# Output projections and down-projections finished tile by tile, with the norms of finished tiles in half rows between products of later tiles

## Chip, cores and metric

One core of one Trainium2 chip. The metric is the device time in microseconds of one execution, as the median of several runs of the same program; lower is better.

## What is computed

A decoder trunk of two layers over 512 tokens of width 1024, float32. Every sub-layer is `x + post_norm(f(pre_norm(x)))` with RMS norms over the 1024 columns; f is a mixer (recurrent heads in layer 0, sparse attention in layer 1) or a squared-ReLU MLP of width 4096. Cut to what matters here:

```python
def rmsnorm(x, w):
    return x * lax.rsqrt(jnp.mean(x * x, axis=-1, keepdims=True) + 1e-6) * w
x = x + rmsnorm(mixer(rmsnorm(x, pre_mix)) @ w_out, post_mix)       # w_out 1024 x 1024
u = rmsnorm(x, pre_ffn)
x = x + rmsnorm(jnp.square(relu(u @ w_up)) @ w_down, post_ffn)      # 1024 x 4096, 4096 x 1024
```

## The kernel before

Tokens stand in four tiles of 128 partitions (i = 0 to 3, NT); the residual is `xres`. Every large product is made of three float32r products (`mm3`, L307 to L311): each operand is split into a high part (ACT copies it, rounding) and a low part (DVE subtracts the high part). SyncE streams 200 weight chunks of 128 x 1024 (512 KB) into a ring of four slots; a slot is loaded again when its chunk's low part has been made (`w_lo`, `stream`). `split_hi` (ACT, L294) and `split_lo` (DVE, L302) make `wh` and `wl`, also four slots each; they wait until PE has used the chunk four places earlier (`w_used`).

The program is a row of stages, each written for every engine separately and in fixed order; `meet` is a barrier of PE, ACT, DVE and POOL between them. Inside a stage each engine runs its own list in order and waits on semaphores. `Chain.link` and `Chain.sig` also make an engine wait for its own last result.

- `oproj_pe` (L1376): for every one of eight chunks k, all four tiles and both halves of 512 columns, so 24 products a chunk into eight PSUM banks (bank 2i + h for tile i, half h). All tiles end in the last chunk.
- `post_act`, `post_dve` (L376, L385): the post-norm of a tile, whole rows: ACT squares and sums `ffo[i]` and takes the root; DVE takes the reciprocal, scales by it and the row `rowbuf` (L393) and adds to `xres` (L395).
- `norm_act`, `norm_dve`, `norm_pe` (L337, L355, L318): the pre-norm: ACT squares `xres[i]` and takes the root, DVE writes `utok` (L365, two buffers), PE turns it by eight 128 x 128 transposes (L328), ACT and DVE write high and low parts `uh`, `ul` (L342, L360).
- `first_hi`, `first_lo`: the next stage's first two chunks are split behind that.
- `mlp_pe`, `mlp_act`, `mlp_dve` (L1441 to L1524): two passes (`it`) over half of the 4096 hidden columns each. Each pass has 16 chunks of up-projection (24 products each), then eight chunks of down-projection for the left 512 output columns in banks 4 to 7 and eight for the right ones in banks 0 to 3, every chunk for all four tiles; DVE adds the banks into `ffo`, which POOL cleared before (L2064, L2075). Only inside the last chunk do the tiles end one after another.

The four places that the prediction speaks of are: output projection of layer 0 to its MLP; end of that MLP to the input projection of layer 1 (`proj1`, operands `uh`, `ul`, `wh`, `wl` of its own, `D1`, of which the input part lies over buffers that the MLP uses); output projection of layer 1 to its MLP; end of that MLP to the output. `DM` names the MLP's and output projection's four operand buffers.

Of the kernel before, what the change touches and what calls it, by code (L numbers as in the profile page):

```python
# [29 lines left out]
P = 128  # L30
# [115 lines left out]
def program(nc, wstream, x, pos, params, consts, rows, out):  # L146
    with ExitStack() as ctx:
# [22 lines left out]
        st = sb("st", [P, 32])  # L170
# [76 lines left out]
        utok = sb("utok", [P, 2, D], c=ml)  # L247
        sb("rest", [P, 2 * HF * T - 2 * D], c=ml)
# [4 lines left out]
        DM = [uh_m, ul_m, wh_m, wl_m]  # L253
        hraw = sb("hraw", [P, 2, T], c=ml)
# [36 lines left out]
        def split_hi(a, dn, c, it=0, per=0):  # L291
            a.e.wait_ge(slot_sems[c % RING], it * (16 * per // RING) + 16 * (c // RING + 1))
            a.e.wait_ge(sem("w_used"), it * per + c + 1)
            a.sig(a.e.activation(dn[2][:, c % RING, :], slot(c), ACT.Copy), sem("w_hi"), it * per + c + 1)  # L294
# [20 lines left out]
        NORM_TURN = (0, 2, 3, 5)  # L315


        def norm_pe(pe, c, ut):  # L318
            if c == 2:
                pe.wait_ge(sem("right_out"), 12)  # L320
            elif c % 2:

                pe.wait_ge(sem("ffo_left"), 4 * (c // 2) + 4)
                pe.wait_ge(sem("ffo_right"), 4 * (c // 2) + 4)
            for i in range(NT):
                pe.wait_ge(sem("norm_u"), 4 * c + i + 1)
# [10 lines left out]
        def norm_act(a, c, dn, ut):  # L337
            def high(i):
                a.e.wait_ge(sem("turned"), 4 * NORM_TURN[c] + i + 1)
                for h in range(2):  # L340
                    hi, _, src = turned(dn, i, h)
                    a.sig(a.e.activation(hi, src, ACT.Copy), sem("high_done"), 8 * NORM_TURN[c] + 2 * i + h + 1)  # L342
            for i in range(NT):
                if c > 0:
                    a.e.wait_ge(sem("x_updated"), 4 * (c - 1) + i + 1)
                if i >= 2:
                    a.e.wait_ge(sem("turned"), 4 * NORM_TURN[c] + i - 1)
                a.link(a.e.activation(ut[:, i % 2, :], xres[:, i, :], ACT.Square, accum_out=st[:, i:i + 1]))
                a.sig(a.e.activation(st[:, 4 + i:5 + i], st[:, i:i + 1], ACT.Sqrt, bias=eps, scale=1.0 / D),
                      sem("norm_root"), 4 * c + i + 1)  # L350
# [4 lines left out]
        def norm_dve(v, c, dn, ut, row):  # L355
            def low(i):
                for h in range(2):
                    hi, lo, src = turned(dn, i, h)
                    v.e.wait_ge(sem("high_done"), 8 * NORM_TURN[c] + 2 * i + h + 1)
                    v.link(v.e.tensor_tensor(lo, src, hi.bitcast(F32), ALU.subtract))  # L360
            v.e.wait_ge(sem("pre_loaded"), 16 * (c + 1))
            for i in range(NT):
                v.e.wait_ge(sem("norm_root"), 4 * c + i + 1)
                v.link(v.e.reciprocal(st[:, 8 + i:9 + i], st[:, 4 + i:5 + i]))
                v.sig(v.e.scalar_tensor_tensor(ut[:, i % 2, :], xres[:, i, :], st[:, 8 + i:9 + i], row[:, :], ALU.mult, ALU.mult),  # L365
                      sem("norm_u"), 4 * c + i + 1)
# [6 lines left out]

        def post_act(a, c, ready, scratch):  # L376
            for i in range(NT):
                ready(i)
                if i >= 2:
                    a.e.wait_ge(sem("post_root"), 4 * c + i - 1)  # L380
                a.link(a.e.activation(scratch(i), ffo[:, i, :], ACT.Square, accum_out=st[:, 16 + i:17 + i]))
                a.sig(a.e.activation(st[:, 20 + i:21 + i], st[:, 16 + i:17 + i], ACT.Sqrt, bias=eps, scale=1.0 / D),
                      sem("post_root"), 4 * c + i + 1)

        def post_dve(v, c, ready):  # L385
            v.e.wait_ge(sem("row_loaded"), 16 * (c + 1))
            ready(0)
            for i in range(NT):
                if i + 1 < NT:
                    ready(i + 1)  # L390
                v.e.wait_ge(sem("post_root"), 4 * c + i + 1)
                v.link(v.e.reciprocal(st[:, 24 + i:25 + i], st[:, 20 + i:21 + i]))
                v.link(v.e.scalar_tensor_tensor(ffo[:, i, :], ffo[:, i, :], st[:, 24 + i:25 + i], rowbuf[:, :],  # L393
                                                ALU.mult, ALU.mult))
                v.sig(v.e.tensor_tensor(xres[:, i, :], xres[:, i, :], ffo[:, i, :], ALU.add),  # L395
                      sem("x_updated"), 4 * c + i + 1)

# [975 lines left out]
        def oproj_pe(pe, first):  # L1376
            mh, ml_, wh, wl = DM
            for k in range(KD):
                c = first + k
                weights(pe, c)  # L1380
                for i in range(NT):
                    if k == KD - 1 and i > 0:
                        ins.then_inc(sem("tile_done"), 1)
                    t = slice(i * P, (i + 1) * P)
                    for h in range(2):
                        w = slice(h * 512, (h + 1) * 512)
                        ins = mm3(pe, bank[2 * i + h][:, :], mh[:, k, t], ml_[:, k, t], wh[:, c % RING, w], wl[:, c % RING, w], k == 0, k == KD - 1)
                ins.then_inc(sem("w_used"), 1)

        def row_in(act, r):  # L1390
            act.dma_start(rowbuf[:, :], rows[r:r + 1, :].to_broadcast([P, D])).then_inc(sem("row_loaded"), 16)

        def oproj_act(a, c, first):
            if c == 0:

                a.e.dma_start(xres[:, :, :], x_d).then_inc(sem("aux_loaded"), 16)
            row_in(a.e, 2 * c)
            pre_in(a.e, 2 * c + 1, prerow)
            for k in range(KD):
                split_hi(a, DM, first + k)  # L1400

            def ready(i):
                if i < NT - 1:
# [869 lines left out]
```

## Time and profile before

| | |
|---|---|
| median of 3 runs | 1752.99 us (1751.8 to 1754.39) |
| the profiled execution | 1752.1 us, of which 1750.3 us span |
| mean granted TensorE clock | 0.931 of full speed |
| PE, DVE, ACT, POOL busy | 87%, 49%, 38%, 6% of the span |
| DMA | 119.42 MB, mean 68 GB/s |

Busy time is a share over the whole program. The timeline lists instructions in order of start with their length; what stands in brackets is how long the engine had been idle before and which instruction on which engine released it. Products overlap: each is recorded with 0.39 us, and the distance of two starts is what one costs. PEclk is the granted TensorE clock, 1.0 being the upper level (2.4 GHz) and 0.5 the lower (1.2 GHz).

### The profile page before, as it was taken

How to read it: one execution, taken by the hardware profiler on the slowest of the kernel's cores; microseconds unless marked ns; L12 is line 12 of the kernel's file. 1: busy time of each engine (PE TensorE's matmuls, PEld its weight loads, DVE VectorE, ACT ScalarE, POOL GpSimd, SP SyncE). 2: the span in 40 equal slices, each digit the busy share in tenths (PEclk: the TensorE clock that was granted, in tenths of full speed). 3: DMA queues.
4: the chain of work that ended last, by engine and by line, in shares of the span. 5: the costliest groups of instructions: out<-in, count | busy, mean ns of one | idle time of the engine just before them, and what ended most of it. 6: DMA issues, size and time to landing. Idle time of an engine off the chain costs nothing.

```text
span 1750.3 us, 22860 instructions
## 1 busy us (share of the span) xinstructions
PE 1528.7 (87%) x8817; PEld 1269.1 (73%) x8817; DVE 864.4 (49%) x1356; ACT 663.4 (38%) x1116; POOL 99.1 (6%) x133
## 2 busy tenths in 40 slices
PE   3999988998929499999997796779979599999996
PEld 2776766887828388888885685669977488888885
DVE  3366636656481644224424425577761644224423
ACT  3544413444441444114412324347762444124411
POOL 0100012212150000000000000000000000000000
PEclk8999988999959699999999797789989699999998
DMA  5222200000023223222321231200011123322321
GB/s 193 73 79 78 73 0 1 1 1 1 8 106 116 72 95 110 97 83 94 113 97 37 72 97 47 73 1 2 2 57 65 60 97 109 96 85 96 109 84 48
DMA packets 32260, 119.42 MB, mean 68 GB/s; under 512 B 3616, under 2 KB 3616, under 8 KB 32032
## 3 DMA queue, kind: packets, MB, share of 16 engines
q1 hardware_dynamic: 29616, 109.10, 18.9%
q10 hardware_dynamic: 2544, 8.92, 1.4%
q8 instruction: 71, 1.16, 0.3%
q14 instruction: 29, 0.24, 0.0%
HBM read 115.91 MB, written 2.10 MB: 67 GB/s over the span
## 4 chain that ended last, share of the span: by engine, by line
PE 57%; DVE 6%; ACT 2%; issue 1%; ACTq 0%; DVEq 0%
PE bank L309 16%; PE bank L310 16%; PE bank L311 16%; PE bank L1928 2%; PE bank L1941 2%; PE bank L1918 1%; PE bank L1917 1%; PE bank L1777 1%; DVE ffo L393 1%; DVE xres L395 1%; PE bank L1807 1%; PE bank L1919 1%; PE bank L328 0%; PE bank L1823 0%; DVE utok L365 0%
## 5 line engine op out<-in xcount | busy, mean ns | idle before, releaser
L302 DVE TENSOR_TENSOR wl_m<-ring,wh_m 128x1024 fp32r<-128x1024 f32 x144 | 176.5, 1226 | 226.5 <-ACT wh_m L294 225.2
L294 ACT ACTIVATE wh_m<-ring 128x1024 fp32r<-128x1024 f32 x144 | 152.8, 1061 | 278.2 <-PE bank L311 264.4
L309 PE MATMUL bank<-uh_m,wh_m 128*128 128x512 f32 x512 | 201.3, 393 | 12.5 <-DVEq L1496 10.6
L310 PE MATMUL bank<-ul_m,wh_m 128*128 128x512 f32 x512 | 200.7, 392 | 0.0
L311 PE MATMUL bank<-uh_m,wl_m 128*128 128x512 f32 x512 | 200.4, 391 | 0.0
L309 PE MATMUL bank<-wh_m,hh 128*128 128x512 f32 x512 | 199.2, 389 | 0.0
L310 PE MATMUL bank<-wl_m,hh 128*128 128x512 f32 x512 | 199.2, 389 | 0.0
L311 PE MATMUL bank<-wh_m,hl 128*128 128x512 f32 x512 | 199.2, 389 | 0.0
L1505 DVE TENSOR_TENSOR hraw<-hraw 128x512 f32<-128x512 f32 x64 | 44.3, 693 | 171.0 <-ACT hraw L1483 171.0
L1483 ACT ACTIVATE hraw<-bank 128x512 f32<-128x512 f32 x64 | 38.3, 598 | 221.9 <-PE bank L311 221.9
L309 PEld LDWEIGHTS bank<-uh_m,wh_m 128*128 128x128 f32 x512 | 97.0, 189 | 34.1 <-POOLq L259 5.7
L311 PEld LDWEIGHTS bank<-uh_m,wl_m 128*128 128x128 f32 x512 | 97.1, 190 | 20.4
L310 PEld LDWEIGHTS bank<-ul_m,wh_m 128*128 128x128 f32 x512 | 97.1, 190 | 20.2
L311 PEld LDWEIGHTS bank<-wh_m,hl 128*128 128x128 f32 x512 | 96.1, 188 | 20.0
L309 PEld LDWEIGHTS bank<-wh_m,hh 128*128 128x128 f32 x512 | 96.1, 188 | 19.9
L310 PEld LDWEIGHTS bank<-wl_m,hh 128*128 128x128 f32 x512 | 96.1, 188 | 19.9
L302 DVE TENSOR_TENSOR wl<-ring,wh 128x1024 fp32r<-128x1024 f32 x47 | 58.1, 1236 | 105.7 <-ACT wh L294 105.5
L309 PE MATMUL bank<-uh,wh 128*128 128x512 f32 x216 | 87.9, 407 | 5.1 <-DVEq L259 5.1
L310 PE MATMUL bank<-ul,wh 128*128 128x512 f32 x216 | 85.4, 395 | 0.0
L311 PE MATMUL bank<-uh,wl 128*128 128x512 f32 x216 | 85.4, 395 | 0.0
L1975 ACT ACTIVATE pb<-bank,nmax 128x128 f32<-128x128 f32 (+3 forms) x128 | 64.3, 530 | 27.9 <-DVE nmax L1991 27.4
L328 PE MATMUL bank<-con,utok 128*128 128x128 f32 x96 | 21.6, 409 | 52.8 <-DVE utok L365 52.8
(380 smaller groups left out, 2799.0 us busy)
## 6 DMA issues: line engine op xcount, KB each, us to landing
ring<-in_wstream_dram SPq DMA_DIRECT2D x200, 512.0 KB, 3.4
rowbuf<-in_rows_dram ACTq DMA_DIRECT2D x6, 512.0 KB, 6.9
xres<-in_x_dram SPq DMA_DIRECT2D x1, 2048.0 KB, 12.0
xres<-in_x_dram ACTq DMA_DIRECT2D x1, 2048.0 KB, 7.4
out_dram<-xres ACTq DMA_DIRECT2D x4, 512.0 KB, 3.2
prerow<-in_rows_dram ACTq DMA_DIRECT2D x3, 512.0 KB, 8.4
con<-in_consts_dram SPq DMA_DIRECT2D x1, 1127.5 KB, 7.4
par<-in_params_dram SPq DMA_DIRECT2D x1, 955.5 KB, 13.9
```

The costliest lines, as they stand in the source:

```text
L294: a.sig(a.e.activation(dn[2][:, c % RING, :], slot(c), ACT.Copy), sem("w_hi"), it * per + c + 1)
L302: v.sig(v.e.tensor_tensor(dn[3][:, c % RING, :], slot(c), dn[2][:, c % RING, :].bitcast(F32), ALU.subtract), sem("w_lo"), it * per + c + 1)
L309: pe.matmul(out, lh, rh, start=start, stop=False)
L310: pe.matmul(out, lh, rl, start=False, stop=False)
L311: return pe.matmul(out, ll, rh, start=False, stop=stop)
L328: ins = pe.transpose(bank[2 * i + k // 4][:, (k % 4) * P:(k % 4 + 1) * P], ut[:, i % 2, k * P:(k + 1) * P], ident)
L393: v.link(v.e.scalar_tensor_tensor(ffo[:, i, :], ffo[:, i, :], st[:, 24 + i:25 + i], rowbuf[:, :], ALU.mult, ALU.mult))
L1483: a.sig(e.activation(hraw[:, s % 2, :], bank[s % 4][:, :], ACT.Relu), sem("relu_done"), it * HF + (hb + s + 1))
L1505: v.sig(e.tensor_tensor(h, h, h, ALU.mult), sem("h_sq"), it * HF + (hb + s + 1))
L1928: ins = pe.transpose(bank[4 + i % 2][:, k * P:(k + 1) * P], pb[:, i, k * P:(k + 1) * P], ident)
L1941: ins = pe.matmul(bank[6 + b][r:r + 64, i * (HD + 1):(i + 1) * (HD + 1)], pT[:, g % 2, c:c + 64], vx[:, k, b, h % KG, :], start=(k == 0), ...
L1975: e.activation(pb[:, i, 0:w], bank[i][:, 0:w], ACT.Exp, bias=nmax[:, g % 2, i:i + 1]).then_inc(sem("p_sb"), 1)
```

## The change

1. Output projection: all eight chunks stay split in memory (`o_weights`: four in `DM`, four in new buffers `wh_o`, `wl_o` over the hidden activations' place). PE makes tiles 0 and 1 over all chunks, then tile 2, then the left half of tile 3, then transposes tiles 0 and 1, then the right half of tile 3, then transposes tiles 2 and 3.
2. The last half of each down-projection (right columns, second pass) likewise: the last four of eight chunks are split into `DD`, the memory of `uh_m` and `ul_m`. Tiles 0 and 1, tile 2, (first MLP: transposes of 0 and 1), tile 3, (transposes of 2 and 3).
3. Norms in half rows: ACT squares 512 columns at a time, for an output projection straight out of PSUM; an Identity step turns the first half's sum into the bias of the root over the second half's. DVE multiplies by `rowbuf` without waiting for the root, and one scalar_tensor_tensor per half scales by 1/root and adds to `xres`. The copy of the output projection into `ffo` goes. `ffo` takes the place of `utok`.
4. Both next chunks' splits stand inside the last tile's norm. POOL's clearings of `ffo` go; the first pass copies the banks instead of adding them.

The core of it:

```diff
+        def turn_tile(pe, n, i):
+            for h in range(2):
+                pe.wait_ge(sem("u_new"), 8 * n + 2 * i + h + 1)
+                for q in range(4):
+                    ins = pe.transpose(bank[TURN_BANK[n][i] + h][:, q * P:(q + 1) * P], ffo[:, i, (4 * h + q) * P:(4 * h + q + 1) * P], ident)
+                ins.then_inc(sem("n_turned"), 1)
+
+        def post_half(a, i, h, src, event, value):
+
+            a.sig(a.e.activation(hraw[:, h, :], src, ACT.Square, accum_out=ST(4 + h, i)), sem(event), value)
+            if h == 0:
+                a.link(a.e.activation(ST(6, i), ST(4, i), ACT.Identity, bias=eps, scale=1.0 / D))
...
+        def x_out(v, n, i, scaled):
+            v.e.wait_ge(sem("post_root"), 4 * n + i + 1)
+            v.link(v.e.reciprocal(ST(8, i), ST(7, i)))
+            for h in range(2):
+                x = xres[:, i, half(h)]
+                v.sig(v.e.scalar_tensor_tensor(x, scaled(i, h), ST(8, i), x, ALU.mult, ALU.add), sem("x_new"), 8 * n + 2 * i + h + 1)
...
             for k in range(KD):
-                c = first + k
-                weights(pe, c)
-                for i in range(NT):
-                    if k == KD - 1 and i > 0:
+                weights(pe, first + k)
+                for i in range(2):
+                    for h in range(2):
+                        ins = product(i, h, k)
+                    if k == KD - 1:
                         ins.then_inc(sem("tile_done"), 1)
...
+            for h in range(2):
+                for k in range(KD):
+                    ins = product(2, h, k)
+            ins.then_inc(sem("tile_done"), 1)
             for k in range(KD):
+                ins = product(3, 0, k)
+            ins.then_inc(sem("tile_done"), 1)
+            turn_tile(pe, n, 0)
+            turn_tile(pe, n, 1)
             for k in range(KD):
+                product(3, 1, k).then_inc(sem("w_used"), 1)
+            turn_tile(pe, n, 2)
+            turn_tile(pe, n, 3)
...
+            post(0)
+            post(1)
+            pre_root(a, n, 0)
+            pre_root(a, n, 1)
+            post(2)
+            pre_root(a, n, 2)
+            high_out(a, DM, n, 0)
+            high_out(a, DM, n, 1)
+            post(3)
+            for c in range(2):
+                split_hi(a, DM, first + KD + c)
+            pre_root(a, n, 3)
+            high_out(a, DM, n, 2)
+            high_out(a, DM, n, 3)
...
+            for f in range(HF):
+                ins = down(2, f, 2, first + HF + J + f // 2, d_weights(f // 2))
+            ins.then_inc(sem("tile_done"), 1)
+            if c == 0:
+                turn_tile(pe, 1, 0)
+                turn_tile(pe, 1, 1)
+            for f in range(HF):
+                ins = down(3, f, 3, first + HF + J + f // 2, d_weights(f // 2))
+                if f % 2:
+                    ins.then_inc(sem("w_used"), 1)
...
+            post(3)
+            if c == 0:
+                used(e, first + 2 * MB - 1)
+                high_out(a, D1, n, 0)
+                high_out(a, D1, n, 1)
+                pre_root(a, n, 3)
+                for k in range(2):
+                    split_hi(a, D1, C_IN1 + k)
+                high_out(a, D1, n, 2)
+                high_out(a, D1, n, 3)
...
+            def scale(i):
+                r = ffo[:, i, half(1)]
+                d_ready(e, first, c, i)
+                v.sig(e.tensor_tensor(r, bank[i][:, :], r, ALU.add), sem("right_sum"), 4 * c + i + 1)
+                v.link(e.tensor_tensor(scaled(i, 1), r, rowbuf[:, half(1)], ALU.mult))
...
-            pool.wait_ge(sem("x_updated"), 4)
-            g.link(pool.memset(ffo[:, :, :], 0.0))
```

PE at the first output projection's end, before: the last products (`uh_m` is here the mixer's output), all transposes, the first products of the MLP.

```order
L309 MATMUL bank<-wh_m,uh_m 128x512
L310 MATMUL bank<-wl_m,uh_m 128x512
L311 MATMUL bank<-wh_m,ul_m 128x512
L328 MATMUL bank<-con,utok 128x128 x32
L309 MATMUL bank<-uh_m,wh_m 128x512
L310 MATMUL bank<-ul_m,wh_m 128x512
L311 MATMUL bank<-uh_m,wl_m 128x512
```

The same stage on PE after the change, the transposes of tiles 0 and 1 with their neighbours:

```order
L313 MATMUL bank<-wl_o,uh_m 128x512
L314 MATMUL bank<-wh_o,ul_m 128x512
L386 MATMUL bank<-con,ffo 128x128 x16
L312 MATMUL bank<-wh_m,uh_m 128x512
L313 MATMUL bank<-wl_m,uh_m 128x512
L314 MATMUL bank<-wh_m,ul_m 128x512
```

And the transposes of tiles 2 and 3, between the last product and the MLP's first:

```order
L313 MATMUL bank<-wl_o,uh_m 128x512
L314 MATMUL bank<-wh_o,ul_m 128x512
L386 MATMUL bank<-con,ffo 128x128 x16
L312 MATMUL bank<-uh_m,wh_m 128x512
L313 MATMUL bank<-ul_m,wh_m 128x512
```

Sixteen of the 32 transposes have moved in front of the last 24 products; sixteen stay behind them.

DVE there, before, from the last tile's post-norm (L392 to L395) through the pre-norms (L365), the low parts (L360) and the splits (L302):

```order
L392 RECIPROCAL st<-st 128x1
L393 SCALAR_TENSOR_TENSOR ffo<-ffo,st,rowbuf 128x1024
L395 TENSOR_TENSOR xres<-xres,ffo 128x1024
L364 RECIPROCAL st<-st 128x1
L365 SCALAR_TENSOR_TENSOR utok<-xres,st,prerow 128x1024
L364 RECIPROCAL st<-st 128x1
L365 SCALAR_TENSOR_TENSOR utok<-xres,st,prerow 128x1024
L360 TENSOR_TENSOR ul_m<-bank,uh_m 128x4x128 x2
L364 RECIPROCAL st<-st 128x1
L365 SCALAR_TENSOR_TENSOR utok<-xres,st,prerow 128x1024
L360 TENSOR_TENSOR ul_m<-bank,uh_m 128x4x128 x2
L364 RECIPROCAL st<-st 128x1
```

After the change, from the last pre-norm step of tile 2 (L425) to the end of the stage:

```order
L425 SCALAR_TENSOR_TENSOR ffo<-xres,st,prerow 128x512 x2
L432 TENSOR_TENSOR ul_m<-bank,uh_m 128x4x128 x4
L1492 TENSOR_TENSOR ffo<-bank,rowbuf 128x512 x2
L305 TENSOR_TENSOR wl_m<-ring,wh_m 128x1024
L416 RECIPROCAL st<-st 128x1
L419 SCALAR_TENSOR_TENSOR xres<-ffo,st,xres 128x512 x2
L305 TENSOR_TENSOR wl_m<-ring,wh_m 128x1024
L423 RECIPROCAL st<-st 128x1
L425 SCALAR_TENSOR_TENSOR ffo<-xres,st,prerow 128x512 x2
L432 TENSOR_TENSOR ul_m<-bank,uh_m 128x4x128 x4
```

The post-norms and pre-norms of three tiles and the low parts of two stand ahead of the last tile's scaling (L1492); behind it are the last tile's x (L419) and u (L425), both weight splits, and four low parts (L432).

DVE at the first MLP's end, after the change (L1670 adds the right half, L1671 multiplies it by the row into PSUM):

```order
L1670 TENSOR_TENSOR ffo<-bank,ffo 128x512
L1671 TENSOR_TENSOR bank<-ffo,rowbuf 128x512
L416 RECIPROCAL st<-st 128x1
L419 SCALAR_TENSOR_TENSOR xres<-ffo,st,xres 128x512
L419 SCALAR_TENSOR_TENSOR xres<-bank,st,xres 128x512
L432 TENSOR_TENSOR ul<-bank,uh 128x4x128 x4
L423 RECIPROCAL st<-st 128x1
L425 SCALAR_TENSOR_TENSOR ffo<-xres,st,prerow 128x512 x2
L305 TENSOR_TENSOR wl<-ring,wh 128x1024 x2
L432 TENSOR_TENSOR ul<-bank,uh 128x4x128 x4
```

Here all eight low parts (L432) stand behind the last tile's sum, where the order before is that of the output projection's end, with the buffers of `D1`.

## Rows read from the trace of the kernel before

**Rows 1.** Page, parts 1 (busy us, share, instructions) and 4 (chain by engine)

```profile
PE 1528.7 (87%) x8817; PEld 1269.1 (73%) x8817; DVE 864.4 (49%) x1356; ACT 663.4 (38%) x1116; POOL 99.1 (6%) x133
...
PE 57%; DVE 6%; ACT 2%; issue 1%; ACTq 0%; DVEq 0%
```

**Rows 2.** Waits of PE: engine line waited for: us in total, times, longest us

```profile
PE bank L328 <- DVE utok L365: 52.8, 9, 14.5
...
PE bank L309 <- DVEq L1496: 10.6, 2, 5.3
```

**Rows 3.** Timeline of PE, first output projection to MLP: start, length, operation

```profile
568.05 0.39 PE L310 MATMUL bank<-wl_m,uh_m 128*128 128x512 f32 x1
568.28 0.39 PE L311 MATMUL bank<-wh_m,ul_m 128*128 128x512 f32 x1
...
581.89 3.65 PE L328 MATMUL bank<-con,utok 128*128 128x128 f32 x16 [13.22 <-DVE utok L365]
...
588.30 1.10 PE L328 MATMUL bank<-con,utok 128*128 128x128 f32 x8 [2.77 <-DVE utok L365]
...
591.27 1.97 PE L328 MATMUL bank<-con,utok 128*128 128x128 f32 x8 [1.87 <-DVE utok L365]
...
598.54 0.76 PE L309 MATMUL bank<-uh_m,wh_m 128*128 128x512 f32 x1 [5.30 <-DVEq L1496]
...
603.33 0.40 PE L311 MATMUL bank<-uh_m,wl_m 128*128 128x512 f32 x1
```

**Rows 4.** Timeline of PE, around first MLP's end and second output projection's end

```profile
949.99 0.39 PE L311 MATMUL bank<-wh_m,hl 128*128 128x512 f32 x1
...
979.44 0.79 PE L309 MATMUL bank<-wh,uh 128*128 128x512 f32 x1 [5.10 <-DVEq L259]
...
1353.37 0.39 PE L311 MATMUL bank<-wh_m,ul_m 128*128 128x512 f32 x1
...
1384.92 0.76 PE L309 MATMUL bank<-uh_m,wh_m 128*128 128x512 f32 x1 [5.30 <-DVEq L1496]
```

**Rows 5.** Timelines of PE and DVE, the end of the program

```profile
1735.80 0.39 PE L311 MATMUL bank<-wh_m,hl 128*128 128x512 f32 x1
...
1745.91 1.23 DVE L395 TENSOR_TENSOR xres<-xres,ffo 128x1024 f32<-128x1024 f32 x1
```

**Rows 6.** Windows of the first gap: us, then busy us by engine, PEclk, DMA

```profile
568.70:582.00 13.30, 0.11 (x1) 0.14 (x2) 12.75 (x17) 7.36 (x17) 1.66 (x1) 0.64 0.00 0
582.00:594.00 12.00, 6.61 (x32) 5.57 (x32) 8.31 (x11) 7.11 (x14) 1.86 (x1) 0.64 0.01 2
```

**Rows 7.** Timeline of ACT, first output projection's norms and splits

```profile
565.51 1.06 ACT L381 ACTIVATE utok<-ffo 128x1024 f32<-128x1024 f32 x1 [0.23 <-DVE ffo L1422]
...
566.69 0.29 ACT L382 ACTIVATE st<-st,con 128x1 f32<-128x1 f32 x1
...
583.93 1.23 ACT L342 ACTIVATE uh_m<-bank 128x512 fp32r<-128x512 f32 x2 [4.68 <-PE bank L328]
...
594.59 2.14 ACT L294 ACTIVATE wh_m<-ring 128x1024 fp32r<-128x1024 f32 x2
```

**Rows 8.** Timeline of DVE, same place and the half rows just before

```profile
511.85 0.75 DVE L1359 SCALAR_TENSOR_TENSOR ul_m<-bank,par,uh_m 128x512 fp32r<-128x512 f32 x1
...
567.70 0.17 DVE L392 RECIPROCAL st<-st 128x1 f32<-128x1 f32 x1 [0.93 <-ACT ffo L1407]
...
584.63 1.42 DVE L360 TENSOR_TENSOR ul_m<-bank,uh_m 128x512 fp32r<-128x512 f32 x2 [1.36 <-ACT uh_m L342]
...
595.75 2.48 DVE L302 TENSOR_TENSOR wl_m<-ring,wh_m 128x1024 fp32r<-128x1024 f32 x2 [0.30 <-ACT wh_m L294]
```

**Rows 9.** Weight ring from 521 to 540 us: issue to landing

```profile
DMA to landing us min/median/max: 3.3/7.6/7.6
```

**Rows 10.** Timeline of DVE, last MLP, behind the left half's products

```profile
1692.77 2.87 DVE L1516 TENSOR_TENSOR ffo<-bank,ffo 128x512 f32<-128x512 f32 x4 [8.48 <-PE bank L311]
1695.67 2.48 DVE L302 TENSOR_TENSOR wl_m<-ring,wh_m 128x1024 fp32r<-128x1024 f32 x2
```

More of the change, by code:

```diff
@@ L353, in norm_act, with norm_dve @@
             high(NT - 1)
[L355 removed]
+        def norm_dve(v, dn, ut, row):
             def low(i):
@@ L385, in post_dve, with row_in @@
[L385 to L396, printed above, removed]
+        def row_in(act, r):
+            act.dma_start(rowbuf[:, :], rows[r:r + 1, :].to_broadcast([P, D])).then_inc(sem("row_loaded"), 16)
@@ new lines, in u_out, with low_out @@
+        def u_out(v, n, i):
+            v.e.wait_ge(sem("pre_root"), 4 * n + i + 1)
+            v.link(v.e.reciprocal(ST(13, i), ST(12, i)))
+            for h in range(2):
+                v.sig(v.e.scalar_tensor_tensor(ffo[:, i, half(h)], xres[:, i, half(h)], ST(13, i), prerow[:, half(h)], ALU.mult, ALU.mult),
+                      sem("u_new"), 8 * n + 2 * i + h + 1)
+        def low_out(v, dn, n, i):
+            for h in range(2):
+                hi, lo, src = renorm_out(dn, n, i, h)
+                v.e.wait_ge(sem("n_high"), 8 * n + 2 * i + h + 1)
+                v.link(v.e.tensor_tensor(lo, src, hi.bitcast(F32), ALU.subtract))
@@ new lines, in mlp_pe @@
+                for j in range(J):
+                    ch = first + HF + j
+                    weights(pe, ch, it, MB)
+                    pe.wait_ge(sem("h_lo"), it * HF + (2 * HF * c + 2 * j + 2))
+                    for f in (2 * j, 2 * j + 1):
+                        for i in range(NT):
+                            ins = down(i, f, 4 + i, ch)
+                    ins.then_inc(sem("w_used"), 1)
+                for j in range(J):
+                    ch = first + HF + J + j
+                    weights(pe, ch, it, MB)
+                    for f in (2 * j, 2 * j + 1):
+                        for i in range(NT if it == 0 else 2):
+                            ins = down(i, f, i, ch, d_weights(j) if it else None)
+                            if it == 1 and f == HF - 1:
@@ L1509, in mlp_dve @@
                         e.sem_inc(sem("hraw_free"), 1)
[L1510 to L1511 removed]
+                    for right, end in ((0, HF + J - 1), (1, MB - 1)):
+                        if s == end:
                             used(e, first + s, it, MB)
                             for i in range(NT):
[L1514 to L1516 removed]
@@ new lines, in mlp_dve @@
+                                if right:
+                                    v.sig(ins, sem("right_out"), 8 * c + 4 + i + 1)
+                                else:
+                                    v.sig(ins, sem("left_out"), it * 4 + (12 * c + 4 + i + 1))
+            for j in range(2, J):
+                split_lo(v, [None, None] + list(d_weights(j)), first + HF + J + j, 1, MB)
+            e.wait_ge(sem("row_loaded"), 16 * (n + 1))
+            for i in range(NT):
+                e.wait_ge(sem("left_sq"), 4 * c + i + 1)
+                v.link(e.tensor_tensor(ffo[:, i, half(0)], ffo[:, i, half(0)], rowbuf[:, half(0)], ALU.mult))
```

318 lines of the change are left out of this document (182 added, 136 removed).

## The prediction

> **What bounds the kernel now.** I read the page first. TensorE (PE) is busy for 1528.7 of 1750.3 us and the chain that ended last is 57% PE, nearly all of it in the three-product helper [rows 1]: in the large products nothing but PE sets the time. Then the list of PE's waits. Its longest total, 52.8 us in 9 waits, is for the token rows that VectorE (DVE) writes in the pre-norm, and 10.6 us more is for the stage barrier that follows [rows 2]. The timeline shows where that lies. At the end of the first output projection the last product starts at 568.28 and the first product of the MLP at 598.54, 30.26 us later; between them PE does 32 transposes and otherwise waits [rows 3]. The same gap is 979.44 - 949.99 = 29.45 us after the first MLP and 1384.92 - 1353.37 = 31.55 us after the second output projection [rows 4]. After the last MLP there is no product left: 1750.3 - 1735.80 = 14.5 us from the last product's start to the end of the span [rows 5]. Together 105.8 us, in which DVE works almost without a break (12.75 of 13.30 us in the first part of the first gap [rows 6]). So the four junctions are bound by DVE and ScalarE (ACT), and products are bound by PE: the change can only win by putting junction work beside products.
>
> **The prices.** Two products in succession start 0.227 us apart at full clock (568.05, 568.28) [rows 3]. ACT: a square of a whole row with its sum 1.18 (565.51 to 566.69, when the root starts), the root 0.29, so 0.33 with the handover [rows 7]; two half rows out of PSUM 1.23, so 0.63 each, and two weight splits 2.14, so 1.08 each with the handover. DVE: a reciprocal 0.17; two half-row subtractions 1.42, so 0.73 each; a half-row scalar_tensor_tensor 0.75, so 0.78; two weight splits 2.48, so 1.24 each [rows 8]. A square of a half row is not in the trace: it lies between 0.62 (a half-row copy) and 1.18 (the whole row with its sum), and I take 0.78: the whole-row square alone (1.06) is as long as a whole-row split (1.07), so half a row should be near the half-row copy, and the sum comes on top. DVE writing its product into PSUM (the right half of the down-projection) isn't there either: the nearest row is the half-row subtraction that reads PSUM, 0.73; I take that, and twice that as the upper bound; nothing there excludes a little less.
>
> **Inside the products: what is added to PE.** Sixteen of the 32 transposes of each of the three junctions now stand between products. Eight took 1.10 us at full clock and 1.97 at half [rows 3]; after products the clock is full, so 16 cost 2.2 us (upper bound 4.0). The product count is unchanged, only the order. Three junctions: 6.6 us added.
>
> Do tiles 0 and 1 reach these transposes in time? In the output projection DVE has four scalings (2.9), and per tile two passes of reciprocal and two half rows (2 x 2 x 1.76 = 7.0), plus about 1.2 of waiting for ACT: 11.1 us after tile 1's last product, while PE has 48 + 24 products, 16.3 us, in front of the transposes. In the down-projection it is 9.9 us against 48 products, 10.9 us. No stall, though the second margin is thin.
>
> Do the weights come in time? A chunk now lasts 12 products, 2.7 us, in the passes over tiles 0 and 1, where it lasted 24 (5.4). Splits take 1.24 a chunk on DVE. In the worst window a refill landed 7.6 us after its issue [rows 9]; with four slots that is (7.6 + 1.1 + 1.2) / 4 = 2.5 us a chunk. In the down-projection DVE first adds four left halves, then splits the third chunk: 2.9 + 1.3 = 4.2 us after the left products ended (1692.77 to 1696.9 in this trace [rows 10]), needed at 5.4. So nothing is added. The two clearings of ffo on POOL go; they lay beside the junctions. The first accumulation becomes a copy at the same length. ACT's extra work (small Identity steps, two per tile at 0.33) falls mostly beside products. Each costs nothing while PE is in products.
>
> **The junctions after the change**, from the last product's start (its result is usable about 0.5 us later).
>
> Output projection (twice). ACT's last square 0.8 to 1.3, root to 1.7, first split to 2.7. DVE's second split half waits for that and ends at 4.0; then reciprocal and x in two halves to 5.8. The second weight split keeps DVE until 7.05; beside it ACT squares both halves of x and takes the root, to 7.0. Reciprocal and two half rows: 8.8. PE transposes the first half from about 8.1, both by 10.3, at half clock. ACT's high part of the second half to 11.0, DVE's low part to about 12.1, barrier and first product 0.3: **12.4 us**. Gain: 30.26 - 12.4 - 2.2 = 15.7 in the first, 31.55 - 12.4 - 2.2 = 16.95 in the second (there a table load also leaves the exposed part).
>
> First MLP. The buffer for the next layer's input overlaps the weights in use, so the high and low parts of tiles 0 to 2 may only start after the last product, and DVE is the bound: sum and scaling 1.45, wait for the root 0.5, reciprocal and x 1.76, low parts of tiles 0 and 1 2.9, reciprocal and u 1.76, two splits 2.5, low parts of tiles 2 and 3 2.9: 13.8, with the start and barrier **14.6 us**. Gain 29.45 - 14.6 - 2.2 = 12.65.
>
> End of the program. Sum 0.73, square 0.78 (beside the scaling), root 0.33, reciprocal 0.2, two half rows 1.56, handovers: 4.2 us from the last product's start, then the output transfer as now, from 1747.14 to 1750.3, 3.2 [rows 5]: **7.4 us**, gain 7.1.
>
> Sum: 15.7 + 16.95 + 12.65 + 7.1 = 52.4 us. The profiled execution took 1752.1, which gives 1699.7; the median is 0.9 higher, 1752.99, which gives **1700.6 us**.
>
> The clock at the restarts I leave as it is. After the gap the products start at half clock: 11 intervals took 4.79 us (598.54 to 603.33) where full clock needs 2.5 [rows 3], 2.3 us lost per junction. The first such start came after 5.30 us without work on PE; the new gaps still hold some 6 us of it, and about 2 more before the first product.
>
> **A rule against the change.** In the stretch from 582 to 594 us PE did only transposes, and the granted clock averaged 0.64 there; eight of them ran at 1.10 us after 16 others [rows 3, 6]. So in this trace the clock rose on transposes alone. The Trainium skill (TensorE: Matmul & The Clock Gate, Part 4: PE-mode transpose) says the opposite, that transpose-mode work doesn't count as PE being busy and the full clock doesn't engage. By the rule the transposes between products would work like idle time; by the row they don't.
>
> **Rivals.**
> 1. The 16 transposes among products drop the clock and the products behind them restart at half: three times 2.3 = 6.9 us lost, 1707.5. For: PE goes from dense products to short operations, and what one such interruption does to the clock the trace doesn't show. Against: the clock rose on transposes, and in the 13.3 us after the last product, with nothing on PE, it still averaged 0.64 [rows 6], so it did not fall at once. This is what the skill's rule above would bring. Chance 0.08.
> 2. The shorter gaps keep the clock up to the next products: 6.9 us won, 1693.7. For: transposes right behind the last product, and a gap of 12 where it was 30. Against: 6 us of silence in its middle, where 5.30 us were followed by a start at half clock. 0.08.
> 3. The pieces don't fit beside the products as walked: the half-row chain is slower (squares at 1.18, four per tile, handovers), PE stands at the in-line transposes of the MLP, and the tails grow. With 0.5 us more on each of some five path squares or writes per junction, and 1 to 2 us of standing in the first MLP, 10 us less is won: 1710.6. It would also be what one sees if the norm work didn't overlap as the change says. 0.10.
> 4. Slower than before: the weights become the bound. Four passes take 8 chunks each at half the old time per chunk. It decides from 52.4 / 32 = 1.64 us of lateness per chunk, 4.3 us in place of 2.7, a refill round of 17 us over the four slots; at 19 us (4.75 a chunk, 2.05 late) it costs 66 us: 1766. For: 3.1 MB of x and rows load during the first of these passes. Against: 7.6 us was the slowest landing even then, and half of the chunks are loaded before the pass begins. 0.02.
>
> **Numbers.** The forecast as walked has 0.72. Its unknown costs: up to 0.7 us for writing PSUM at two ends, 0.4 more for some three exposed squares at each of four junctions (4.8), 1.8 for each set of in-line transposes (5.4): upper end 1700.6 + 1.4 + 4.8 + 5.4 = 1712; with not all at once, and the rivals 1 and 3, I close at 1711. The lower end takes in rival 2, 1693.7, so 1694. A measurement of this kernel can tell about 0.2% (3.5 us) from no change; all cases but the last and a piece of it lie far below: faster 0.97, same 0.01, slower 0.02.
>
> **What would show it.** Right: PE's gaps between the last product and the next stage near 12.4, 14.6 and 12.4 us and 7.4 at the end; two groups of 16 transposes at each junction, the first within products and about 2.2 us long; no PE wait for split weights inside the two-tile passes; DVE in the first MLP's gap without a break. Wrong: products at 0.427 us pitch behind the in-line transposes (rival 1), full clock from the first product of a stage (2), a wait of PE for ffo ahead of the in-line transposes or gaps over 15 us (3), waits for the split weights (4). If the gaps agree and the time doesn't, the order of products has a price that I set at nothing.

## The result and the profile after

| | before | after |
|---|---|---|
| median | 1753.03 us (4 runs) | 1701.57 us (4 runs, 1701.43 to 1702.56) |
| ratio, 95% interval | | 0.9707 [0.9691, 0.9724] |
| span of the profiled execution | 1750.3 us | 1699.7 us |
| mean granted clock | 0.931 | 0.948 |

The forecast was 1700.6 us, with a range from 1694 to 1711. Busy times and the last chain by engine, from the page (answers to [rows 1]; the chain shown is the one from the last instruction back and here reaches less far):

```profile
PE 1522.0 (90%) x8817; PEld 1263.8 (74%) x8817; DVE 868.5 (51%) x1392; ACT 674.4 (40%) x1192; POOL 91.6 (5%) x131
...
PE 23%; DVE 1%; ACT 0%; issue 0%; ACTq 0%; DVEq 0%
```

PE is busy for 6.7 us less in a span that is 50.6 us shorter. Its waits for the token rows and for the stage barrier (answers to [rows 2]; engine, line, waited for: us in total, times, longest):

```profile
PE bank L386 <- DVE ffo L425: 20.8, 3, 7.0
...
PE bank L312 <- DVEq L1634: 3.9, 2, 2.0
```

52.8 us in nine waits have become 20.8 in three, and 10.6 at the barrier 3.9. Timeline of PE around the first output projection's end (answers to [rows 3]):

```profile
565.49 0.40 PE L314 MATMUL bank<-wh_o,ul_m 128*128 128x512 f32 x1
565.72 1.91 PE L386 MATMUL bank<-con,ffo 128*128 128x128 f32 x16
567.38 0.48 PE L312 MATMUL bank<-wh_m,uh_m 128*128 128x512 f32 x1
567.70 0.39 PE L313 MATMUL bank<-wl_m,uh_m 128*128 128x512 f32 x1
...
572.73 0.39 PE L314 MATMUL bank<-wh_o,ul_m 128*128 128x512 f32 x1
572.96 1.04 PE L386 MATMUL bank<-con,ffo 128*128 128x128 f32 x8
580.96 1.97 PE L386 MATMUL bank<-con,ffo 128*128 128x128 f32 x8 [6.97 <-DVE ffo L425]
584.90 0.77 PE L312 MATMUL bank<-uh_m,wh_m 128*128 128x512 f32 x1 [1.97 <-DVEq L1634]
...
588.38 0.40 PE L314 MATMUL bank<-uh_m,wl_m 128*128 128x512 f32 x1
```

Sixteen transposes stand among the products and move the next product from 565.72 to 567.38, by 1.66 us. The products behind them are at full clock at once. From the last product's start (572.73) to the MLP's first (584.90) it is 12.17 us, where it was 30.26. The start is at half clock again: eight intervals until 588.38 took 3.48 us.

PE at the first MLP's end and at the second output projection's end (answers to [rows 4]):

```profile
937.53 0.39 PE L314 MATMUL bank<-uh_m,hl 128*128 128x512 f32 x1
...
951.91 0.79 PE L312 MATMUL bank<-wh,uh 128*128 128x512 f32 x1 [4.29 <-DVEq L261]
...
1327.49 0.39 PE L314 MATMUL bank<-wh_o,ul_m 128*128 128x512 f32 x1
...
1339.66 0.76 PE L312 MATMUL bank<-uh_m,wh_m 128*128 128x512 f32 x1 [1.97 <-DVEq L1634]
```

951.91 - 937.53 = 14.38 us (29.45 before) and 1339.66 - 1327.49 = 12.17 us (31.55). The window from the last product to the last tile's first transposes in the first gap (us, then busy us of PE, PEld, DVE, ACT, POOL, PEclk, DMA share; answers to [rows 6]):

```profile
573.00:581.00 8.00, 1.03 (x10) 0.80 (x8) 5.78 (x9) 6.21 (x13) 0.00 (x0) 0.82 0.21 71
```

DVE is busy for 5.78 of 8.00 us and ACT for 6.21, where DVE had 12.75 of 13.30 and ACT 7.36: what is left is one tile's chain to and fro between them.

ACT in the pass over tiles 0 and 1 (the fifth chunk's split) and at the last half row of tile 3 (answers to [rows 7]):

```profile
532.18 1.06 ACT L297 ACTIVATE wh_o<-ring 128x1024 fp32r<-128x1024 f32 x1 [5.29 <-DMA ring<-in_wstream_dram]
...
573.22 0.60 ACT L391 ACTIVATE hraw<-bank 128x512 f32<-128x512 f32 x1 [3.27 <-PE bank L314]
...
573.94 0.29 ACT L396 ACTIVATE st<-st 128x1 f32<-128x1 f32 x1
```

The fifth chunk's split came when its transfer landed, 532.18, and PE first used that chunk at 538.51: the weights were in time. A half-row square took 0.60, and the root started 0.72 after it. DVE from the last half row on (answers to [rows 8]):

```profile
574.00 0.69 DVE L1492 TENSOR_TENSOR ffo<-bank,rowbuf 128x512 f32<-128x512 f32 x1 [2.26 <-ACT hraw L391]
575.42 1.23 DVE L305 TENSOR_TENSOR wl_m<-ring,wh_m 128x1024 fp32r<-128x1024 f32 x1 [0.72 <-ACT wh_m L297]
576.68 0.16 DVE L416 RECIPROCAL st<-st 128x1 f32<-128x1 f32 x1
576.88 1.54 DVE L419 SCALAR_TENSOR_TENSOR xres<-ffo,st,xres 128x512 f32<-128x512 f32 x2
578.45 1.22 DVE L305 TENSOR_TENSOR wl_m<-ring,wh_m 128x1024 fp32r<-128x1024 f32 x1
```

Between the scaling (574.00) and the reciprocal (576.68) stands a weight split that waits for ACT's half of it. The end of the program (answers to [rows 5]):

```profile
1690.31 0.39 PE L314 MATMUL bank<-uh_m,hl 128*128 128x512 f32 x1
...
1691.53 0.70 DVE L1671 TENSOR_TENSOR bank<-ffo,rowbuf 128x512 f32<-128x512 f32 x1
...
1693.73 0.75 DVE L419 SCALAR_TENSOR_TENSOR xres<-bank,st,xres 128x512 f32<-128x512 f32 x1
...
1692.67 2.91 ACTq L2311 DMA_DIRECT2D out_dram<-xres  x4
```

The last product starts at 1690.31, the span ends at 1699.7: 9.39 us, not 7.4. DVE is done at 1694.48 and has kept to the forecast (4.17 us after the last product's start, forecast 4.2). But ScalarE issued all four output transfers between 1692.67 and 1695.6: they stand in its list behind the last root. Before, they stood behind the last root too:

```profile
1743.17 4.34 ACTq L2158 DMA_DIRECT2D out_dram<-xres  x4
```

From the first issue to the end of the span it was 7.1 us then (1743.17 to 1750.3), and it is 7.0 us now.

### The profile page after: what moved, and what is told of

It reads as the page before. It is cut to its first block and busy times, and to the rows that moved or that the text cites. A ratio compares the mean times of both kernels' runs of the same rounds, so it can differ in the third digit from the quotient of the medians.

```text
span 1699.7 us, 22980 instructions
## 1 busy us (share of the span) xinstructions
PE 1522.0 (90%) x8817; PEld 1263.8 (74%) x8817; DVE 868.5 (51%) x1392; ACT 674.4 (40%) x1192; POOL 91.6 (5%) x131
## 5 line engine op out<-in xcount | busy, mean ns | idle before, releaser
L305 DVE TENSOR_TENSOR wl_m<-ring,wh_m 128x1024 fp32r<-128x1024 f32 x128 | 156.9, 1226 | 161.5 <-ACT wh_m L297 160.3
L297 ACT ACTIVATE wh_m<-ring 128x1024 fp32r<-128x1024 f32 x128 | 135.8, 1061 | 202.0 <-PE bank L314 189.3
L312 PE MATMUL bank<-wh_m,hh 128*128 128x512 f32 x448 | 174.4, 389 | 0.0
L314 PE MATMUL bank<-wh_m,hl 128*128 128x512 f32 x448 | 174.3, 389 | 0.0
L313 PE MATMUL bank<-wl_m,hh 128*128 128x512 f32 x448 | 174.3, 389 | 0.0
L314 PEld LDWEIGHTS bank<-wh_m,hl 128*128 128x128 f32 x448 | 84.1, 188 | 17.6
L313 PEld LDWEIGHTS bank<-wl_m,hh 128*128 128x128 f32 x448 | 84.1, 188 | 17.4
L312 PEld LDWEIGHTS bank<-wh_m,hh 128*128 128x128 f32 x448 | 84.1, 188 | 17.4
L312 PE MATMUL bank<-wh,uh 128*128 128x512 f32 (+1 forms) x160 | 62.0, 387 | 4.3 <-DVEq L261 4.3
```

The lines of the kernel that those rows point to most:

```text
L305: v.sig(v.e.tensor_tensor(dn[3][:, c % RING, :], slot(c), dn[2][:, c % RING, :].bitcast(F32), ALU.subtract), sem("w_lo"), it * per + c + 1)
L312: pe.matmul(out, lh, rh, start=start, stop=False)
L313: pe.matmul(out, lh, rl, start=False, stop=False)
L314: return pe.matmul(out, ll, rh, start=False, stop=stop)
```

## The experiments

Gaps below are from the start of a stage's last product to the start of the next stage's first. All times compare with the kernel before, run on the same chip beside it.

**1. Tiles together again in the output projections.**

```diff
             for k in range(KD):
                 weights(pe, first + k)
-                for i in range(2):
+                for i in range(NT):
                     for h in range(2):
                         ins = product(i, h, k)
...
+                ins.then_inc(sem("w_used"), 1)
+            for i in range(NT):
+                turn_tile(pe, n, i)
```

> Output projections only: PE goes back to all four tiles chunk by chunk, transposes all behind the last product; the half-row norms and the MLP stay as changed. Theory (the gain is work moved beside products, half rows by themselves win little): the gap from the last product's start to the MLP's first rises from 12.2 to about 29 us at both places, minus 1.7 us for the transposes that leave the products: +15.3 us each, near 1732 us. Rival (the gain is that half-row norms have a shorter chain, whatever the order of products): the gap stays under 20 us, +3 to +12 us in all, 1705 to 1714.

Measured 1732.44 us, ratio 0.9877 [0.9862, 0.9892]. PE:

```profile
570.91 0.39 PE L314 MATMUL bank<-wh_o,ul_m 128*128 128x512 f32 x1
576.53 3.87 PE L386 MATMUL bank<-con,ffo 128*128 128x128 f32 x16 [5.23 <-DVE ffo L425]
584.91 1.97 PE L386 MATMUL bank<-con,ffo 128*128 128x128 f32 x8 [4.52 <-DVE ffo L425]
595.57 1.97 PE L386 MATMUL bank<-con,ffo 128*128 128x128 f32 x8 [8.69 <-DVE ffo L425]
599.51 0.76 PE L312 MATMUL bank<-uh_m,wh_m 128*128 128x512 f32 x1 [1.97 <-DVEq L1624]
```

The gap is 599.51 - 570.91 = 28.60 us; at the second place it is 1370.85 - 1340.96 = 29.89. So half rows as such, with the new order inside ACT's and DVE's lists, take 1.66 us off either gap (30.26, 31.55; the second is 1.29 longer in both kernels, where a table load of ScalarE, 1.28 us, stands just ahead of it). The rest of the gain there comes from the order of products, by which the norms of three tiles run beside products. The rival falls. The same was not tried at the first MLP's end: how much of its 15.07 us is half rows and how much is order is not shown.

**2. Outputs issued by SyncE.**

```diff
             stream(sp)
+            for i in range(NT):
+                sp.wait_ge(sem("x_new"), 24 + 2 * i + 2)
+                sp.dma_start(out_d[:, i, :], xres[:, i, :]).then_inc(sem("x_moved"), 16)
...
-            for i in range(NT):
-                act.wait_ge(sem("x_new"), 24 + 2 * i + 2)
-                act.dma_start(out_d[:, i, :], xres[:, i, :]).then_inc(sem("x_moved"), 16)
```

> The four output transfers are issued by SyncE, each as soon as its tile of x is ready, in place of by ScalarE behind its last root. Theory (the tail of 9.4 us, 2.0 over what was forecast, is the 2 MB that all start moving only at 1692.7): the tail falls to about 7.2 us, time 1699.5. Rival (the tail is the fixed cost of the last transfer and its wait): tail stays at 9.4, 1701.6.

Measured 1699.47 us, 0.9695 [0.9681, 0.9708]. PE's last product, and the four issues (1672.30 is the first, the second number the stretch to the end of the last):

```profile
1689.56 0.39 PE L314 MATMUL bank<-uh_m,hl 128*128 128x512 f32 x1
...
1672.30 21.79 SPq L2218 DMA_DIRECT2D out_dram<-xres  x4
```

The span ends at 1696.9, 7.34 us after the last product's start. A transfer lands 2.7 us after its issue at the median, where it was 4.0 with all four at once. That accounts for the 2.05 us by which the tail was too long: it was bound by 2.1 MB, which in the changed kernel moved at 401 to 418 GB/s from 1694 to 1698, so in some 5 us, and could not start before ScalarE came to them. The gap shows this, not the median: the unaltered kernel did not run beside this one, and the runs scatter from 1697.26 to 1700.95 us.

**3. The MLP's in-line transposes behind the last product.**

```diff
             ins.then_inc(sem("tile_done"), 1)
-            if c == 0:
-                turn_tile(pe, 1, 0)
-                turn_tile(pe, 1, 1)
             for f in range(HF):
...
             if c == 0:
-                turn_tile(pe, 1, 2)
-                turn_tile(pe, 1, 3)
+                for i in range(NT):
+                    turn_tile(pe, 1, i)
```

> First MLP only: the 16 transposes of tiles 0 and 1 stand behind the last product instead of before tile 3. Theory (behind it DVE is the bound and PE waits about 7 us, so they are free there, and cost 1.7 us among the products): gap from last product to next stage unchanged at 14.4, time 1699.9. Rival (the high parts start later and everything shifts): gap longer by 1.7 or more, 1701.6 or above.

Measured 1700.34 us (five runs, 1696.16 to 1702.44), 0.9698 [0.9684, 0.9711]. PE:

```profile
933.74 0.39 PE L314 MATMUL bank<-uh_m,hl 128*128 128x512 f32 x1
933.97 2.78 PE L386 MATMUL bank<-con,ffo 128*128 128x128 f32 x24
941.86 1.97 PE L386 MATMUL bank<-con,ffo 128*128 128x128 f32 x8 [5.11 <-DVE ffo L425]
948.12 0.79 PE L312 MATMUL bank<-wh,uh 128*128 128x512 f32 x1 [4.29 <-DVEq L261]
```

948.12 - 933.74 = 14.38 us, to the hundredth what it was with 16 of them moved in front: here they are free behind the last product and cost 1.67 us among products. The shape in the profile is the one expected; the time agrees within its scatter and by itself proves nothing.

**4. The output projections' in-line transposes behind the last product.** The same edit in `oproj_pe`, without experiment 3.

```diff
-            turn_tile(pe, n, 0)
-            turn_tile(pe, n, 1)
             for k in range(KD):
                 product(3, 1, k).then_inc(sem("w_used"), 1)
-            turn_tile(pe, n, 2)
-            turn_tile(pe, n, 3)
+            for i in range(NT):
+                turn_tile(pe, n, i)
```

> Output projections only: the 16 transposes of tiles 0 and 1 stand behind the last product. Theory (there the high and low parts of tiles 0 and 1, 2.9 us on DVE, then join the path together with the last tile's scaling, which comes behind them on ScalarE): the gap grows from 12.2 to about 16.6 us at both places, 1.7 us less among products, so +2.7 us each, 1707. Rival (in-line transposes bring nothing, as in the MLP): 1698.

Measured 1707.59 us, 0.9741 [0.9727, 0.9754]. PE, and DVE's low parts of tiles 0 and 1:

```profile
571.03 0.40 PE L314 MATMUL bank<-wh_o,ul_m 128*128 128x512 f32 x1
571.26 2.78 PE L386 MATMUL bank<-con,ffo 128*128 128x128 f32 x24
...
572.66 2.87 DVE L432 TENSOR_TENSOR ul_m<-bank,uh_m 128x512 fp32r<-128x512 f32 x4 [4.43 <-ACT uh_m L412]
...
583.30 1.97 PE L386 MATMUL bank<-con,ffo 128*128 128x128 f32 x8 [9.25 <-DVE ffo L425]
587.24 0.77 PE L312 MATMUL bank<-uh_m,wh_m 128*128 128x512 f32 x1 [1.97 <-DVEq L1632]
```

587.24 - 571.03 = 16.21 us, 4.04 more than 12.17, for 1.66 less among products: +2.4 a place where +2.7 was expected. The same 16 transposes are worth having in-line here and not in the MLP. What decides is not the transposes but what they release: here the high and low parts of two tiles, which now keep DVE from 572.66 to 575.53, ahead of the last tile's scaling at 575.56 (the changed kernel had only the last half row left to scale, at 574.00, 1.27 us after the last product's start). In the MLP these parts wait for the last product anyway.

**5. In-line transposes twice, beside the unaltered kernel.**

```diff
-                for q in range(4):
+                for q in [0, 1, 2, 3] * (2 if i < 2 else 1):
```

> The changed kernel once more, unaltered, beside the next three on the same chip. All theories: 1701.6 us, and the same four gaps (12.2, 14.4, 12.2 and 9.4 us from the last product's start). The time up to the first output projection, 3.1 us longer than before in the profiled execution though nothing there was changed, tells whether that is the change's (then again 525.1 us) or chance (then anywhere between 522 and 526).

> Each of the 16 transposes that stand among products is done twice over. Theory (they cost their own time and don't touch the clock): 3.3 us in place of 1.66 at each of the three places, products behind them 0.227 us apart, 1706.6 us. Rival (longer stretches of transposes count as idle for the clock): products behind them restart 0.427 us apart, 2.3 us more at each place, 1713.

The unaltered kernel: 1700.04 us, 0.9695 [0.9682, 0.9708], the four gaps 12.17, 14.38, 12.17 and 9.4. With doubled transposes: 1705.92 us, 0.9732 [0.9718, 0.9745]. PE there:

```profile
563.19 0.40 PE L314 MATMUL bank<-wh_o,ul_m 128*128 128x512 f32 x1
563.43 3.65 PE L386 MATMUL bank<-con,ffo 128*128 128x128 f32 x32
566.84 0.48 PE L312 MATMUL bank<-wh_m,uh_m 128*128 128x512 f32 x1
567.15 0.39 PE L313 MATMUL bank<-wl_m,uh_m 128*128 128x512 f32 x1
```

From 563.43 to 566.84 it is 3.41 us, twice 1.66 and 0.1, and the products behind stand 0.23 us apart from the second on. Twice as long a run of transposes did not lower the clock, and the rival falls. But this experiment can't tell whether transposes work like idle time, because idle time of that length didn't lower the clock either. Windows of the kernel before, in its first gap (us, then busy us of PE, PEld, DVE, ACT, POOL, PEclk, DMA):

```profile
568.70:572.50 3.80, 0.00 (x0) 0.00 (x0) 3.66 (x5) 2.20 (x7) 0.00 (x0) 1.00 0.00 0
...
581.90:585.50 3.60, 3.60 (x16) 3.24 (x16) 2.17 (x4) 1.51 (x3) 1.96 (x1) 0.50 0.02 5
586.30:588.20 1.90, 0.00 (x0) 0.00 (x0) 1.40 (x2) 1.77 (x5) 0.00 (x0) 1.00 0.00 0
```

For 3.8 us behind the last product PE did nothing and was granted the full clock. The other two rows do bear on the question. After 13.22 us without work PE did 16 transposes at half clock and nothing else, and in the pause behind them, by 586.3, the granted clock was full. Experiment 1's kernel shows the same: 0.50 during its 16 transposes from 576.53 and 1.00 from 580.7 to 583.9. The Trainium skill (TensorE: Matmul & The Clock Gate, Part 4: PE-mode transpose) says that transposes don't count as PE being busy; these two traces disagree.

**6. One weight split ahead of the last half row.** In both output projections, on ACT and DVE alike:

```diff
             def scale(i):
                 for h in range(2):
+                    if i == 3 and h == 1:
+                        split_lo(v, DM, first + KD)
                     e.wait_ge(sem("o_sq"), 4 * n + 2 * i + h + 1)
...
             scale(3)
-            split_lo(v, DM, first + KD)
             x_out(v, n, 3, scaled)
```

> Output projections only: the first of the next stage's two weight splits stands ahead of the last half row of tile 3 on ScalarE and VectorE, where both wait for PE anyway; the second stays. Theory (the first one is on the path, the second is hidden behind ScalarE's squares): gap 12.2 to 10.3 us at both places, 1697.8. Rival (the slot is used too long by PE, so the split waits and delays the last half row): gap 12.2 or more, 1701.6 or above.

Measured 1700.62 us (five runs from 1695.2 to 1700.89), 0.9697 [0.9684, 0.971]. DVE:

```profile
568.81 0.69 DVE L1495 TENSOR_TENSOR ffo<-bank,rowbuf 128x512 f32<-128x512 f32 x1
570.12 1.23 DVE L305 TENSOR_TENSOR wl_m<-ring,wh_m 128x1024 fp32r<-128x1024 f32 x1 [0.62 <-ACT wh_m L297]
571.77 0.69 DVE L1495 TENSOR_TENSOR ffo<-bank,rowbuf 128x512 f32<-128x512 f32 x1 [0.42 <-ACT hraw L391]
572.50 0.16 DVE L416 RECIPROCAL st<-st 128x1 f32<-128x1 f32 x1
```

The split (570.12) now lies in time in which DVE waited for PE, and the reciprocal follows the scaling directly. The gap is 580.72 - 570.49 = 10.23 us, and 10.22 at the second place: the term is right. The median did not show it, so this kernel, the unaltered one and experiment 7's ran once more:

> The early split again: its gaps were 10.23 us as expected, its median was not lower (1700.62, five runs from 1695.2 to 1700.9) than the unaltered kernel's (1700.04). Theory (the time between executions scatters by some 3 us, by how many products at each start of a stage run at half clock and in stages that are the same in all; the median of five was a high one): median 1696 to 1699 now, two gaps of 10.2. Rival (what the shorter gap saves is given back by more products at half clock behind it): again 1700 to 1701, and 10 or more slow products at each of the two starts behind these gaps.

> The changed kernel unaltered, on the same chip as the two others of this call: 1700 to 1701.6 us by all theories; the slow products at the starts of its stages between 6 and 13 each, not the same ones as before.

1698.74 us (0.9688 [0.9675, 0.9701]) against 1701.18 us (0.9706 [0.9693, 0.9719]); the gaps in the profile were 10.23 again. Over ten runs each the means are 1698.7 and 1700.6: 1.8 us won, of 3.9 by the gaps. By the scatter of the twenty runs the 1.8 is uncertain by about 1.5. The profiles agree with it: from the start of the first output projection to the end of the span it is 1172.8 and 1173.1 us in the unaltered kernel and 1170.6 and 1171.3 with the early split, 2.0 less. Something takes the rest back, and the likely place is the starts of the stages. The number of products that ran 0.427 us apart behind the five long pauses (first output projection, first MLP, layer 1's input projection, second output projection, second MLP) was 7, 13, 6, 9, 6 and 8, 13, 6, 9, 6 in the unaltered kernel, and 12, 12, 13, 6, 9 and 7, 10, 12, 14, 13 with the early split: 41 and 42 against 52 and 56, each of the extra ones 0.2 us. That is 2 to 3 us given back. That the shorter pause is the reason is not shown. Experiments 5 and 4 had 51 and 49 such products, with pauses as long as in the unaltered kernel and 4 us longer, and behind one and the same pause of 12.17 us the MLP's start had 7, 8, 11, 13, 13 and 13 in six profiles. Whatever shifts the stages changes the count. A part of both expectations holds: the scatter is there (the first median was a high one), and in these profiles the starts take back about half. That the unaltered kernel's counts would differ from one profile to the next was expected wrongly: they agreed.

**7. Four edits together.** Experiments 2, 3 and 6, and after the first MLP only one chunk split ahead of the barrier:

```diff
             meet(dve, 6)
+            split_lo(v, D1, C_IN1 + 1)
```

> Together: outputs issued by SyncE, the first MLP's transposes behind its last product, the early split of the output projections, and after the first MLP only one chunk split ahead of the barrier (the second behind it). Theory (four separate terms add up): tail 7.3 (-2.05), no in-line transposes in the MLP (-1.67), gaps of 10.3 twice (-3.8), gap after the first MLP 13.1 (-1.25), in all -8.8: 1692.8 us. Rival (they overlap or the clock eats them): 1695 to 1698.

> The four edits together again: 1692.8 by the sum of the terms, 1694.3 measured the first time. Theory (chance of the starts): between these, and 6 to 9 us under the unaltered kernel. Rival (given back at the starts): 1694 to 1696 and at most 6 us under it.

Measured 1694.34 us, 0.9663 [0.9649, 0.9676], and again 1694.42 us, 0.9668 [0.9654, 0.9681]. The four terms are in the first profile as expected: no transposes among the MLP's products, gaps of 10.22 (570.50 to 580.72) and 10.23 (1321.33 to 1331.56), 13.12 after the first MLP (932.59 to 945.71, expected 13.1), tail 7.32 (1683.48 to 1690.8). The sum of 8.8 us came out as 6.4 by the means of ten runs each. The products at half clock were 12, 12, 13, 13, 13 and 11, 12, 13, 12, 12, in all 63 and 60 in place of 41 and 42: about 4 us, more than the 2.4 that are missing. This version is faster than the changed kernel both times (1694.34 against 1700.04 us, 1694.42 against 1701.18), and the single runs don't overlap.

## Why the prediction was right

The measured 1701.57 us lies 1.0 above the forecast. The spans fell by 50.6 us where the sum said 52.4. Term by term, from the profiled executions:

| term | forecast | measured |
|---|---|---|
| first output projection: gap 30.26 to 12.17, 1.66 in-line | 15.7 | 16.4 |
| first MLP: 29.45 to 14.38, 1.67 in-line | 12.65 | 13.4 |
| second output projection: 31.55 to 12.17, 1.66 in-line | 16.95 | 17.7 |
| end: 14.5 to 9.39 | 7.1 | 5.1 |
| sum of these | 52.4 | 52.7 |
| products of the four changed stages (12 fewer at half clock) | 0 | 1.8 |
| everything up to the first output projection, unchanged code | 0 | -3.1 |
| layer 1 up to the second output projection, unchanged code | 0 | -0.8 |

- **What bounds.** Right: outside the four junctions the changed stages gained 1.8 us, and experiment 1 shows for the output projections that the win comes from the overlap. For the first MLP's end and the program's end this is argued from the walk through the steps, which came out within 0.3 us there (14.38 for 14.6, DVE done after 4.17 for 4.2); behind the first MLP DVE stood only 0.51 us for the root, until 939.97, as forecast.
- **Luck.** That the four terms sum to 52.7 for a forecast of 52.4 is luck: three were 0.7 to 0.8 too small, 2.3 together, and the end was 2.0 too large. And the 3.9 us lost in unchanged code were half made up by the 1.8 from products at half clock; the forecast had neither.
- **Prices.** The half-row square was taken at 0.78 and took 0.72 from PSUM; writing into PSUM, at 0.73 with an upper bound of twice that, took 0.70 (1691.53). The in-line transposes were taken at 2.2 us (two separate groups of eight at 1.10 each) and cost 1.66 in one row. Of the 0.7 us by which each of the first three terms was too small, 0.5 is the transposes and 0.2 the gap.
- **Margins.** PE never waited for the rows of tiles 0 and 1, nor for split weights inside the passes. In the first MLP DVE had written tile 1's row at 923.90 and PE came to its transposes at 925.08: 1.2 us to spare, where the prediction had 1.0.
- **The step that failed** is the end of the program: "then the output transfer as now, from 1747.14 to 1750.3, 3.2". Before, the issues began at 1743.17, 4.0 us ahead of DVE's end (1747.14), and more than half of the bytes had moved by then. After the change they begin at 1692.67, only 1.8 us ahead of DVE's end (1694.48): DVE is done sooner, the issues still stand behind ScalarE's last root, and the transfers became the bound. From DVE's end it is 5.2 us, not 3.2. The order of ScalarE's list, which the forecast used for everything else, was not read to its end. Size 2.0 us; experiment 2 removes it.
- **The clock at restarts** was left as it was. Right as a mechanism: rival 2 (no slow start) didn't happen. But the number of products at half clock behind the five pauses that experiment 6 lists is not constant: 14, 10, 14, 14, 7 before, 11, 7, 11, 9, 6 after.
- **Rivals 1, 3 and 4** fell: full clock behind 16 and 32 transposes (which by experiment 5's windows doesn't tell whether transposes work like idle time); gaps of 12 to 14 us; the fifth chunk split 6 us before its use.
- **Unchanged code.** The first output projection began at 522.02 us before and 525.10 after. Most of it is not the change's doing: the same changed code gave 525.10, 525.67 and 526.35, and kernels that differ from it only later gave 522.71, 522.78, 522.85 and 522.90 as well as 525.02 to 526.06. The thirteen profiles fall into two groups, and the kernel before, of which there is one profile, happened to be in the early one. The groups are apart already at the last input product of layer 0 (244.61 to 244.80 against 246.62 to 247.21). Within the early group the changed code is 0.7 to 0.9 us later than before; whether that is the change's is open. The windows from 215 to 232 us of experiment 5's unaltered kernel and of experiment 6 show one part of it, PEclk 0.80 against 0.90:

```profile
215.00:232.00 17.00, 15.85 (x53) 11.39 (x52) 10.59 (x14) 2.60 (x3) 1.23 (x1) 0.80 0.00 0
```

```profile
215.00:232.00 17.00, 15.85 (x60) 11.72 (x60) 10.16 (x14) 2.60 (x3) 1.23 (x1) 0.90 0.00 0
```

In the first, 11 of 24 products of layer 0's last input chunks (from 220.37 on) ran at half clock, in the second (from 219.08) none. Layer 1 up to the second output projection scatters too: 328.44 us in the changed kernel's profile, 326.46 and 326.56 in its two repeats, 327.65 before. So some 2.3 to 3 us of the forecast's error lie in chance, and 2.0 in the end of the program.

## What to carry to other kernels

Where every tile's result depends on a long chain on other engines, give the tensor engine its tiles one after another instead of all together, keep the weights split in memory for it, and pull the chains of the finished tiles beside the products of the next; shortening the chain itself won a tenth of that at the output projections here (1.66 of 18.09 us). When a tail is shortened, read what each queue still holds behind it: the output transfers overlapped only by the order of an engine's list. And a term that the profile confirms to the hundredth can still be half lost in the median; here probably in the products behind a pause, which start at the lower clock level.

## What was not expected of the hardware

How many products behind a pause run at the lower of the two clock levels (1.2 and 2.4 GHz, intervals of 0.427 and 0.227 us) changes from kernel to kernel by as much time as the savings that one looks for here. In three profiles of the changed kernel the counts were 44, 41 and 42 in sum, the last two almost the same at every start; with pauses 1.9 us shorter at two places they were 52 and 56, with four edits 63 and 60. But with the same pauses and doubled transposes there were 51, and with pauses 4 us longer at two places 49. So the pause's length alone does not set the count; no run varied one pause alone over several lengths, and what sets it stays open.
